# A fused two-block transformer on one core: work re-ordered at four borders between sublayers

## The reference, cut to what matters

```
shift, scale, gate = split(silu(c) @ ada_w + ada_b);  gate = 1 + gate
h = x * (1 + scale) + shift
y = mixer_ab(h) | mlp(h) | mixer_c(h) | mlp(h)
x = layer_norm(alpha * x + gate * y) * ln_g + ln_b
mlp(h) = square(relu(h @ w1)) @ w2
```

## Time and profile before

| | |
|---|---|
| runs | 2401.9, 1174.81, 1179.41 us, median 1179.41 |
| profiled execution | 1180.33 us, span 1178.3 us |
| granted TensorE clock, mean | 0.930 |
| busy | PE 1023.6 us (87%), DVE 746.3 (63%), ACT 514.6 (44%), POOL 82.6 (7%) |
| chain that ended last | PE 49%, DVE 21%, DMA 10%, ACT 9% |
| DMA | 204.85 MB, mean 174 GB/s |

### The profile page before, as it was taken

How to read it: one execution, slowest core, us unless ns; L and a number is a source line. 1 busy time by engine, 2 the same in 40 slices (tenths; PEclk the granted TensorE clock), 3 DMA queues, 4 the chain that set the end, 5 groups by cost and what they waited for, 6 DMA issues and landing times.

```text
span 1178.3 us, 14723 instructions
## 1 busy us (share of the span) xinstructions
PE 1023.6 (87%) x5742; PEld 841.2 (71%) x5742; DVE 746.3 (63%) x1143; ACT 514.6 (44%) x815; POOL 82.6 (7%) x53
## 2 busy tenths in 40 slices
PE   4797787999999797998899999969998988797786
PEld 1474555898898566776698988747887767676664
DVE  2464737777877776555676745755546477775464
ACT  1344253442443252554344434335655255556361
POOL 0000000500000040000060000020000000310000
PEclk8897888999999898998999999979999899998897
DMA  9872334669788674332678865624343155440130
GB/s 333 305 285 72 114 137 151 207 229 317 283 288 311 233 250 155 116 105 72 215 240 235 242 198 179 197 89 143 115 135 99 61 172 179 143 143 1 63 107 36
DMA packets 105303, 204.85 MB, mean 174 GB/s; under 512 B 3834, under 2 KB 38100, under 8 KB 105236
## 3 DMA queue, kind: packets, MB, share of 16 engines
q1 hardware_dynamic: 102180, 193.25, 48.6%
q0 software_dynamic: 3056, 10.67, 3.3%
HBM read 202.76 MB, written 1.15 MB: 173 GB/s over the span
## 4 chain that ended last, share of the span: by engine, by line
PE 49%; DVE 21%; DMA 10%; ACT 9%; issue 6%; POOL 3%; SPq 1%; DVEq 0%; ACTq 0%; POOLq 0%
PE bank L1499 10%; PE bank L1500 10%; PE bank L1501 10%; DVE w_lo L1653 6%; ACT w_hi L1178 4%; DMA raw<-in_mlp_w 4%; DMA raw<-in_ada_w 3%; PE bank L1612 3%; PE bank L1553 3%; PE bank L1555 2%; PE bank L1554 2%; PE bank L1574 2%; ACT probs L1354 2%; POOL x L1125 2%; DMA gate_row<-in_ada_b 2%
## 5 line engine op out<-in xcount | busy, mean ns | idle before, releaser
L1653 DVE TENSOR_TENSOR w_lo<-raw,w_hi 128x2048 fp32r<-128x2048 f32 (+2 forms) x134 | 303.7, 2278 | 192.4 <-ACT w_hi L1178 191.6
L1178 ACT ACTIVATE w_hi<-raw 128x2048 fp32r<-128x2048 f32 (+2 forms) x134 | 247.8, 1857 | 187.0 <-PE bank L1501 77.9
L1499 PE MATMUL bank<-w_lo,ht_hi 128*128 128x512 f32 (+1 forms) x544 | 228.5, 420 | 49.4 <-DVE w_lo L1653 27.5
L1500 PE MATMUL bank<-w_hi,ht_hi 128*128 128x512 f32 (+1 forms) x528 | 215.0, 407 | 0.0
L1501 PE MATMUL bank<-w_hi,ht_lo 128*128 128x512 f32 (+1 forms) x528 | 215.0, 407 | 0.0
L1499 PEld LDWEIGHTS bank<-w_lo,ht_hi 128*128 128x128 f32 x544 | 110.1, 202 | 79.2 <-issue 44.5
L1553 PE MATMUL bank<-ht_hi,w_lo 128*128 128x256 f32 x448 | 127.8, 285 | 3.6 <-DVE w_lo L1653 3.6
L1554 PE MATMUL bank<-ht_lo,w_hi 128*128 128x256 f32 x448 | 126.7, 283 | 0.0
L1555 PE MATMUL bank<-ht_hi,w_hi 128*128 128x256 f32 x448 | 126.7, 283 | 0.0
L1501 PEld LDWEIGHTS bank<-w_hi,ht_lo 128*128 128x128 f32 x528 | 105.9, 201 | 23.7
L1500 PEld LDWEIGHTS bank<-w_hi,ht_hi 128*128 128x128 f32 x528 | 106.7, 202 | 21.2 <-issue 0.2
(11 more groups left out here) (222 smaller groups left out, 1362.2 us busy)
## 6 DMA issues: line engine op xcount, KB each, us to landing
raw<-in_mlp_w SPq DMA_DIRECT2D x64, 1024.0 KB, 5.8
raw<-in_ada_w SPq DMA_DIRECT2D x48, 1024.0 KB, 5.5
raw<-in_a_w_in SPq DMA_DIRECT2D x16, 1024.0 KB, 5.2
raw<-in_c_w_in SPq DMA_DIRECT2D x12, 1024.0 KB, 5.8
raw<-in_b_w_in SPq DMA_DIRECT2D x10, 1024.0 KB, 5.0
raw<-in_ple_w_gate SPq DMA_DIRECT2D x8, 1024.0 KB, 5.0
raw<-in_ab_w_in SPq DMA_DIRECT2D x4, 1024.0 KB, 11.2
raw<-in_ab_w_out SPq DMA_DIRECT2D x4, 1024.0 KB, 5.4
```

Of the source, the lines that this page charges most:

```text
L1178: nc.scalar.activation(split_parts(n)[0], raw_tile(t), ACT.Copy).then_inc(high_done, 1)
L1499: nc.tensor.matmul(dst, a_hi[:, c, rows], lo[:, k, :], start=it["first"] and k == 0, stop=False)
L1500: nc.tensor.matmul(dst, a_hi[:, c, rows], hi[:, k, :], start=False, stop=False)
L1653: nc.vector.tensor_tensor(lo, raw_tile(split[n]), hi.bitcast(F32), ALU.subtract).then_inc(low_done, 1)
```

## The change

The items of the list are put in another order at the borders. Nothing is computed in another way, and no weight load changes its place or its slot.

1. The two groups of ada products that stood at the end of a mixer stand behind the transposes of half 0, two of the four behind the transposes of half 1 (borders A and C).
2. In the last product of both MLPs `ahead_by` is smaller, so some w_hi and w_lo come later than y_ln and ln (borders B and D).
3. The columns of sublayer 3 stand in MLP 0 behind the first tile of the last `down`, not in mixer C.
4. In `halves` ScalarE's copy of early tokens is made at the end, and w_hi and w_lo of the next tiles come ahead of the x rows (border D).
5. The bias of the gate row is asked for ahead of the x rows, and at the start first of all rows.

```diff
@@ entered(s), start of an MLP @@
             across(s, 0, (4, 5), ("act", "act"))
             norm_ln(s - 1, 1)
-            if layer < 2:
-                ada_tiles(1, 7)
+            ada_tiles(2, 7)
             part(0)
             across(s, 1, (4, 5), ("act", "dve"))
-            if layer < 2:
-                ada_tiles(1, 7)
+            ada_tiles(2, 7)
@@ down(g) @@
-                    it = add("tokens", tile=t, kc=4, width=512, lhs=("hid", g % 2), off=h * 4, banks=yb[n], ts=(0, 1), ahead_by=3 if g == 3 else None,
+                    it = add("tokens", tile=t, kc=4, width=512, lhs=("hid", g % 2), off=h * 4, banks=yb[n], ts=(0, 1), ahead_by=3 - h if g == 3 else None,
...
+                    if g == 3 and h == 0 and layer == 0:
+                        columns(3, 0)
+                        columns(3, 1)
...
-                             first=False, last=h == 1, cut=hid_cut[3], enter=False, ahead_by=3 - h)
+                             first=False, last=h == 1, cut=hid_cut[3], enter=False, ahead_by=2 + t - h)
@@ last_tiles(s) @@
         y[1](1, 2, ts=(1,))
-        ada_tiles(2, 7)
@@ halves @@
-    def halves(first, s, extra, ends=True):
+    def halves(first, s, extra, resid):
...
-        early = first(1, 0, ts=(0,), cut=cuts["ht", 0][1], ends=ends)
+        early = first(1, 0, ts=(0,), cut=cuts["ht", 0][1], ends=False)
...
-        first(0, 1, ts=(1,))
-        late = first(1, 2, ts=(1,), ends=(1,) if ends else (0, 1))
+        first(0, 2, ts=(1,))
+        prepare(2)
+        if resid:
+            add("resid", s=s - 1)
+        late = first(1, 2, ts=(1,), ends=(0, 1))
@@ mixer C @@
     k0 = k[0](1)
-    columns(3, 0, (7,))
-    columns(3, 1, (7,))
@@ second block @@
-    q0 = halves(q[0], 4, False, ends=False)
-    plan.insert(len(plan) - 1, {"kind": "resid", "s": 3})
+    q0 = halves(q[0], 4, False, True)
@@ GpSimd @@
+            def gate_bias(s):
+                pool.dma_start(gate_row[:, :], R["ada_b"][s // 2, s % 2, 2 * D:3 * D].partition_broadcast(P)).then_inc(gate_in, 16)
...
                     pool.wait_ge(product_done, 8)
+                    gate_bias(0)
...
-                pool.dma_start(gate_row[:, :], R["ada_b"][s // 2, s % 2, 2 * D:3 * D].partition_broadcast(P)).then_inc(gate_in, 16)
...
                 pool.wait_ge(row_in, 32 * (s + 1))
+                if s < 3:
+                    pool.wait_ge(rows_ready, norms[s, 1]["rows"])
+                    gate_bias(s + 1)
                 for t in range(0 if s < 3 else 1, T):
```

More of the change, by code:

```diff
@@ L595, in make_plan @@
     pair[0] = 0
-    q0 = halves(q[0], 2, True)
+    q0 = halves(q[0], 2, True, False)
     roped(q0, 0)
```

## The result

The changed kernel takes **1171.16 us** (median of 20 runs, 1163.15 to 5471.5) against 1177.94 (20 runs) of the kernel before: a ratio of 0.993, 95% interval 0.991 to 0.9951. That is 6.8 us less by the medians, 8.2 by the ratio, where 14.3 were forecast; the range of 1157 to 1175 holds it. One execution here and two of the kernel before took thousands of us and are left out of the ratio. Measured again in a later comparison it gave 0.991, interval 0.9886 to 0.9933. Its profiled execution took 1169.44 us, span 1167.6, mean granted clock 0.927: 10.7 us under the profiled span of before.

A forecast was written before the change was run, and what follows sets the result against it. TensorE's work was taken as the bound, its stops as what can be won. A -3.4, B -7.45, C -3.45 (gate row included) and D 0 sum to -14.3 us from 1180.33: forecast 1165.5, range 1157 to 1175.

The forecast's parts named there:

- A: border from mixer AB to MLP 0: transposes first, so the first product starts earlier, -2.5 us.
- C: border from mixer C to MLP 1: the same gain from the ada products' new place, -2.35 us.
- B: border from MLP 0 to mixer C: order and columns with the DMA cost together, -7.45 us.
- D: border from MLP 1 to block 2: first stop shrinks, next stop eats the gain, 0 (-1.7 to +2.5).
- Rival 4: transposes at A, B and C: six new stops become half-clock returns of 2.5 us each, kernel slower, 1181; chance 0.03.
- The gate row: MLP 0 and MLP 1: earlier request removes TensorE's wait behind the gate row, -0.9 us at A, -1.1 at C.
- Columns in mixer C: mixer C loses the columns and their stop of 6.12 us: -4.5, with +0.5 for the gate row's DMA.
- B, the order: end of MLP 0: u comes 3.25 us earlier, first product of mixer C at 412.1, not 415.55: -3.45.
- rival 1: inside the MLPs: the gain of A and C is given back, 1169 to 1172 us; chance 0.2.
- longer MLPs as a sign of being wrong: both MLPs: the prediction called itself wrong if the MLPs grow; no size given.
- The gain of 1.7 for fast x rows: border D: the favourable bound, -1.7 us, if x rows take 1.22 each.
- One sign: MLP 0 and MLP 1: first product about 2 us nearer to the transposes of half 0 in the changed profile.

The follow-up runs named there:

- e2: the kernel before with only the two groups of ada products moved behind the transposes (A and C): 1174.91 us, ratio 0.9975.
- e3: the kernel before with only the request for the gate's bias set ahead of the x rows: 1176.65 us, ratio 0.9989.
- e7: the kernel before with only the new order of halves: 1178.48 us, ratio 1.0005.
- e4: the kernel before with only the low parts (preparation of the next weights) set back in both MLPs: 1178.02 us, ratio 1.0005.
- e5: the kernel before with ada products, columns and gate request moved together, without low parts or order of halves: 1167.64 us, ratio 0.992.
- e9: the changed kernel without the low parts set back: 1168.10 us, ratio 0.9912.
- e12: e9 with three groups of ada products behind the transposes of half 0 and one behind half 1: 1170.14 us, ratio 0.9927.
- e1: the kernel before with only the columns of sublayer 3 moved into MLP 0: 1168.84 us, ratio 0.9931.
- e11: the changed kernel itself, measured again: 1168.30 us, ratio 0.991.
- e6: the changed kernel with the old order of halves: 1170.15 us, ratio 0.9946.
- e8: the kernel before with low parts set back and columns moved together: 1175.67 us, ratio 0.9982.

## Why the prediction was right, and where it was not

The time lies in the range and the sign is right; the size is half. By the sum's own terms, each as forecast and then as the traces show it:

- **A, -2.5: gave -1.0**, in all seven traces with this order. VectorE's y_ln was the limit, as argued, and the first product started 2.0 earlier against its surroundings (a lead of 3.48 at 205.71, 1.5 before A); the products then ran at the lower clock and gave 1.0 of it back. I held that a stop of 1.77 leaves the clock alone and the new one would be like it. At A stops of 1.70 to 1.97 did not leave it alone (0.50 to 0.58). Rival 4's mechanism is real, but not at six stops: it came at A each time, at B in two of four traces, and at C in e2 alone.
- **C, -2.35: gave -2.4** wherever the clock stayed up. The term was right.
- **The gate row, -0.9 and -1.1: gave -1.1 and -1.3.** At A cause and size are right, since traces without this part have 0 or less there. At C they have 0.3 to 0.9 too, so the part's own share is nearer to 0.7. No cost of the late load of c or of the shared queues can be told from the scatter.
- **Columns in mixer C, -4.5 + 0.5: gave -4.5 to -5.4**, and 1.2 to 1.4 more at the end of mixer C that the sum did not have. The first part is right as argued (the row of 3.57 ends at 452.87 and not at 452.7, which changes nothing), with its half-clock return in it. The second comes with the columns in nine traces of nine and in none of the others; the sum could not see it.
- **B, the order, -3.45: this step failed.** It gave -1.5 up to the first product of mixer C, in all three traces that have the whole of it, and in two of them the 1.5 was lost again right behind. The sum had the order on VectorE right: from u to the first product it had 5.3, and it was 5.2. What it had wrong is TensorE ahead of u. It took 3.7 for the columns and full speed behind them (n = 1 from 394.8, done at about 405.7, where its own numbers give 405.9). In the trace the columns took 4.55 and the 24 products behind them 7.9 for 5.45, the first half of them at a clock of 0.50. In the times of before (those here plus the lead of 1.5 at 380) TensorE was done 3.1 later than forecast; 1.1 of that filled the stop that the sum still had for u, and u and the first product came 2.0 later. Then the stop of 1.92 brought the lower clock once more, for 1.5.
- **What the low parts do at B depends on the columns.** With the columns ahead, u ends 11.1 after the first n = 1 product starts, in eight traces of eight, with the w_lo ahead of y_ln and without it: TensorE sets u. Moving that w_lo behind u cannot make u earlier there, and lengthens the way from the transposes to the first product, 5.06 for 3.73. The steps at B form a square: 2.8 to 3.3 with neither moved (e2, e3, e7), 7.0 with the low parts alone (e4, one trace), 2.9 with the columns alone (e5, e9, e12; 4.5 in e1, where the slow stretch was shorter), 1.5 with both (changed, e11, e6; 3.1 in e8, where it was shorter too). So the low parts win 3.7 to 4.2 alone and cost 1.4 behind the columns. The trace of before itself stands at 0: its stop of 7.54 was 5.2 to 5.9 in the other three traces with this order, so the sum took its size from a trace with a longer stop than most.
- **MLP 0 gives back what A and the gate win** (rival 1, 0.2): not shown. The rest of MLP 0 took 2.2 more than in the trace of before, but 2.8 and 2.2 more in e1 and e7, which have no gain to give back. And a lead or a lag at 380 passes B: e5, e9 and e12 come with -0.04, -0.3 and -5.0, and each gains 2.9. I had named longer MLPs as a sign of being wrong; since all traces but e8 are 0.5 to 2.8 longer there, it is the one trace of before that was quick.
- **D, 0: gave -1.6 to -1.1 of lead, lost.** The order of halves was costed rightly at nothing (e7 +0.5; e6). The loss is the single w_lo that I put at 0.6 to 1.0: with the lows D's step was -1.0 to -2.2 (changed, e11, e4, e6, e8), without them -0.5 to +2.6 (the other eight). The stop of 4.00 instead of 3.0 is the 1.0 forecast; the rest came behind it and varies. The gain of 1.7 for fast x rows did not come, since the x rows and the w_lo beside GpSimd were slow (3.42, and GpSimd's 4.28 for 3.21). The rule of the Trainium skill, page SBUF — State Buffer, section "SBUF: two separate sides", that a VectorE operation with two SBUF inputs and a GpSimd operation that reads SBUF lock each other out, agrees with this trace: GpSimd's operations ended 2.25 after VectorE's, and VectorE's x row 1.1 after GpSimd's.

One sign was put the wrong way round. I wrote that the first product would be 2 nearer to the transposes of half 0; my own sum has it at 203.7 behind transposes at 198.6, 5.1 against 3.8 before, and 5.1 is what the trace has. What comes 2 earlier is the product itself.

The forecast's sum of 14.3 against this pair of traces: 3.45 at B, 1.5 at A and 1.6 at D are missing, and the rest of MLP 0 takes 2.2. The end of mixer C gives 1.2 that was not forecast, the other terms are 1.2 above theirs, and scatter (1.5 ahead of A, 1.2 in the second block) gives 2.7. That makes the 10.7 between the profiles. The medians differ by 6.8, since the profiled executions lie 1.7 below and 2.4 above theirs. The 1171.2 falls into the band of rival 1 (1169 to 1172), but that is chance: what is missing is missing at A, B and D.

**What stays open.** By the traces the low parts set back cost 3 to 4 us once the columns are moved: 1.4 at B and 1.9 to 2.5 at D between kernels that differ in them alone, and 1.5 more behind B where the clock fell. By the times, e8 against e1 says so (-2.1 against -8.1, intervals just apart), e9 against the changed kernel does not (1168.1 against 1168.3). No kernel was shown to be faster than the changed one; e5, e9 and e1 are as fast with less changed. Why the clock falls behind one stop and not behind a like one is not shown.

## What to carry to other kernels

Two changes that take waits from the same stop do not add up: for each, ask which engine arrives last once the other is in, and cost the second against that. Here a shorter chain on VectorE was worth 3.7 to 4.2 us while VectorE was last, and cost 1.4 once TensorE was. Work of about 4 us, with 2 us of lower clock behind it, cost at most 0.5 ahead of a stop of 5 to 6 us. A part of a few us is seen in the steps between same products of many traces long before the median of ten runs shows it; but one trace of before is a poor zero, and its own scatter stands in every step.

## What the hardware showed that was not expected

- 32 one-column products took 3.6 to 4.8 us with TensorE shown busy throughout, and in all eight traces that have them between other products the granted clock fell to 0.50 during them or within 1.4 us behind them; the 24 products behind them took 6.9 to 8.3 us for 5.45. A busy TensorE can come out of such a stretch at the lower of its two levels, 1.2 GHz.
- Stops of nearly the same length brought different clocks: behind 1.70 to 1.97 at A and 1.93 at C (e2) it was 0.50 to 0.58; behind 1.66 to 1.85 at C it was 1.00. At B it fell behind 1.92 (changed) and 1.80 (e6) and stayed at 1.00 behind 1.69 (e11), 1.82 (e8) and 2.14 (e4). In e8 it fell at A behind 1.77 and 0.67, in the order of the kernel before, where all five others, before among them, kept 1.00.
- The same 512 KB gate row landed in 7.7 to 10.3 us (median 9.5) in the trace of before, where it was asked for behind two other rows, and in 3.6 to 4.0 at the borders of the changed kernel, where it was asked for alone (7.2 at the start, where the other rows follow it at once).
